# Start addresses of two activation tensors, act_a and big, modulo 64 bytes of a partition

## The reference

```python
u = rms_norm(h, ln_mix_pre[l])
hq, hf, hi, hg, aq, ak, av = jnp.split(u @ w_in[l], split_at, axis=-1)
...
mixed = jnp.concatenate([o_rec, o_att], axis=-1) @ w_out[l]
h = h + rms_norm(mixed, ln_mix_post[l])
y = conv_gated_mlp(rms_norm(h, ln_ffn_pre[l]), w_up[l], conv_w[l], conv_b[l], w_down[l])
h = h + rms_norm(y, ln_ffn_post[l])
h = h + (p[l] @ w_pe[l]) * jax.nn.sigmoid(h @ w_pg[l])
```

## Time and profile before

| what | value |
|---|---|
| executions | 1771.39, 1771.07, 1771.08 us, median 1771.08 |
| span of the profiled execution | 1769.3 us; the page gives no other time of it |
| median less span | 1.8 us |
| TensorE busy | 1755.0 us, 99% |
| VectorE, ScalarE, GpSimd busy | 1254.6, 942.8, 612.6 us |
| moved by DMA | 326.61 MB, mean 185 GB/s |

### The profile page before, as it was taken

One profiled execution on the slowest core, in us unless ns is written; L12 is line 12 of the kernel. 1 busy time (PEld: TensorE's weight loads), 2 busy tenths in 40 slices (PEclk: granted clock), 3 DMA queues, 4 the chain that ended last, 5 costly groups with the idle time before them and its releaser, 6 DMA issues.

```text
span 1769.3 us, 29586 instructions
## 1 busy us (share of the span) xinstructions
PE 1755.0 (99%) x10201; PEld 1543.0 (87%) x10201; DVE 1254.6 (71%) x1594; ACT 942.8 (53%) x1254; POOL 612.6 (35%) x621
## 2 busy tenths in 40 slices
PE   9999999999999999999999999999999999999997
PEld 7888888888888888888888888888888888888886
DVE  6877777765598777777777644444987788887754
ACT  5544554554476555555555533334655567775532
POOL 1743345556603333111111322221262255550032
PEclk9999999999999999999999999999999999999999
DMA  8444444436565555555555555556455444444453
GB/s 314 176 177 167 165 167 167 167 143 247 184 237 189 189 190 190 190 190 190 190 190 190 169 190 186 194 185 220 168 190 202 167 167 167 167 167 163 169 188 119
DMA packets 51152, 326.61 MB, mean 185 GB/s; under 512 B 5792, under 2 KB 6432, under 8 KB 18464
## 3 DMA queue, kind: packets, MB, share of 16 engines
q1 hardware_dynamic: 49952, 323.86, 50.9%
q10 hardware_dynamic: 1152, 2.11, 0.4%
HBM read 323.85 MB, written 2.10 MB: 184 GB/s over the span
## 4 chain that ended last, share of the span: by engine, by line
PE 97%; DVE 1%; ACT 1%; DMA 0%; issue 0%; ACTq 0%; DVEq 0%
PE ps L1844 59%; PE ps L1845 30%; PE ps_lev L1844 1%; PE ps_sc L1883 1%; PE ps_lev L1919 1%; PE ps_lev L1969 1%; PE ps_t L1873 1%; PE ps_lev L1845 1%; DMA x_in<-in_x_turned 0%; PE bank_b L1974 0%; DVE wlo L993 0%; PE bank_a L1888 0%; DVE o_out L1702 0%; PE bank_a L1894 0%; PE ps_t L2190 0%; ACT whi L480 0%
## 5 line engine op out<-in xcount | busy, mean ns | idle before, releaser
L1844 PE MATMUL ps<-act_a,whi 128*128 128x512 f32 x3056 | 1069.4, 394 | 0.0
L993 DVE TENSOR_TENSOR wlo<-stage,whi 128x2048 fp32r<-128x2048 f32 (+1 forms) x314 | 689.0, 2195 | 245.8 <-ACT whi L480 240.9
L1845 PE MATMUL ps<-act_a,wlo 128*128 128x256 f32 x3056 | 854.3, 280 | 0.0
L1844 PEld LDWEIGHTS ps<-act_a,whi 128*128 128x128 f32 x3056 | 573.8, 188 | 125.6 <-issue 1.0
L480 ACT ACTIVATE whi<-stage 128x2048 fp32r<-128x2048 f32 (+1 forms) x314 | 565.9, 1802 | 122.6 <-DMA stage<-in_w_down 105.0
L1845 PEld LDWEIGHTS ps<-act_a,wlo 128*128 128x128 f32 x3056 | 574.0, 188 | 0.4
L1844 PE MATMUL ps<-big,whi 128*128 128x512 f32 x1536 | 534.4, 392 | 0.0
L1845 PE MATMUL ps<-big,wlo 128*128 128x256 f32 x1536 | 429.3, 280 | 0.0
L487 ACT ACTIVATE small<-ps 128x256 f32<-128x256 f32 x240 | 91.9, 383 | 533.3 <-PE ps L1845 533.2
L1844 PEld LDWEIGHTS ps<-big,whi 128*128 128x128 f32 x1536 | 288.4, 188 | 63.4
L1845 PEld LDWEIGHTS ps<-big,wlo 128*128 128x128 f32 x1536 | 288.4, 188 | 0.1
(11 more groups left out here) (378 smaller groups left out, 1354.5 us busy)
## 6 DMA issues: line engine op xcount, KB each, us to landing
stage<-in_w_a SPq DMA_DIRECT2D x166, 1024.0 KB, 4.8
stage<-in_w_b SPq DMA_DIRECT2D x86, 1024.0 KB, 4.8
stage<-in_w_down SPq DMA_DIRECT2D x64, 704.0 KB, 4.0
stage<-in_w_a SPq DMA_DIRECT2D x8, 256.0 KB, 8.7
mem_raw<-in_memT SPq DMA_DIRECT2D x1, 2048.0 KB, 9.3
mem_again<-in_memT SPq DMA_DIRECT2D x1, 2048.0 KB, 9.1
x_in<-in_x_turned ACTq DMA_DIRECT2D x7, 256.0 KB, 9.4
x_in<-in_xT SPq DMA_DIRECT2D x3, 512.0 KB, 5.8
```

The source lines that it names most:

```text
L993: dve.tensor_tensor(wlo[:, slot, part], stage[:, slot, part], whi[:, slot, part].bitcast(F32), ALU.subtract).then_inc(w_lo, 1)
L1844: pe.matmul(dst, whi[:, slot, c * P:(c + 1) * P], act, start=start, stop=False)
L1845: return pe.matmul(dst[:, T:2 * T], wlo[:, slot, c * P:(c + 1) * P], act[:, 0:T], start=False, stop=stop)
```

## The change

The start of `act_a` is rounded up to 64 bytes: it moves from 106272 to 106304 (1661 x 64). `big` becomes a view into a row with 16 bytes of padding on either side, and moves from 139040 to 139088 (2173 x 64 + 16). `big_at`, on which the tensors laid over `big` stand, moves from 139040 to 139104, 64 bytes on, so these keep their place modulo 64; only `mem_raw` and `xg` are laid 32 bytes lower and go from 32 to 0 modulo 64. What lies over `act_a` moves with it, from 32 to 0. The end is 229216 of 229344. No instruction, wait or order changes.

```diff
--- before.py
+++ after.py
@@ -148,16 +148,17 @@
         upb = over("upb", conv_at, 0, [P, 2, T + 2])
         cy = over("cy", conv_at, 2080, [P, 2, T])
         gl = over("gl", conv_at, 4128, [P, T])
-        at[0] = conv_at + 4128 + 1024
+        at[0] = (conv_at + 4128 + 1024 + 63) // 64 * 64
         a_at = at[0]
         act_a = sb("act_a", [P, KT, 2 * T], F32R)
-        big_at = at[0]
-        big = sb("big", [P, FT, 2 * T], F32R)
+        big_row = sb("big", [P, 8 + FT * 2 * T], F32R)
+        big = big_row[:, 4:4 + FT * 2 * T].rearrange("p (k t) -> p k t", t=2 * T)
+        big_at = at[0] - 4 * FT * 2 * T
         KB = 1024
 
 
-        mem_raw = over("mem_raw", big_at, 0, [P, KT, T])
-        xg = over("xg", big_at, 16 * KB, [P, KT, T])
+        mem_raw = over("mem_raw", big_at - 32, 0, [P, KT, T])
+        xg = over("xg", big_at - 32, 16 * KB, [P, KT, T])
         warm = over("warm", big_at, 85 * KB, [P, 2 * T], BF16)
         squares = over("squares", big_at, 64 * KB, [P, KT, T])
         xs_mix = big[:, 0:KT, :]
```

## The result

The changed kernel takes 1798.7 us (median of 4 runs, 1798.45 to 1798.92), the kernel before 1771.24 (4 runs). The ratio is 1.0154, with a 95% interval of 1.0142 to 1.0166: slower by 27.5 us. The prediction said 1740.3 and a range up to 1798.

What follows compares the result with a forecast made beforehand. TensorE's matmul pairs were taken to bound the kernel. From a 1769.3 us span, 30.8 us for `act_a` and 0 for `big` left 1738.5, plus 1.8 to the median: 1740.3 us, range 1676 to 1798.

Steps and rivals of the forecast that it cites:

- What bounds the kernel: Whole kernel: TensorE, busy 1755.0 of 1769.3 us and hardly waiting; 4672 matmul pairs at 346.7 ns make 1620 us.
- The excess: Pairs on `act_a` and `big`: 19.7 ns each over 327 ns, 92.0 us in all, that a start address could bear on.
- `act_a` from 32 to 0: Pairs on `act_a`: no 64-byte piece is cut, half the excess goes, 9.85 ns a pair, 30.4 us gained.
- the sixteen matmuls of line 2190 under 233 ns: 512-column matmuls on `act_a`: a pace below 233 ns each was named as a sign of the forecast.
- `big` from 32 to 16: 1584 pairs on `big`: pieces still straddle a border, so 0; bounds 31.2 us of gain or loss.
- Everything laid over them: VectorE and ScalarE work on the moved tensors: no cost of place found, so no change.
- the DMA: The 2 MB DMA into `mem_raw`: stays at a multiple of 32, so nothing changes.
- `xg`: Half-speed float32 streams on `xg`, moved to 0: pace stays about 215 ns, so nothing changes.
- what is late next: Up projection: VectorE's share rises from 78% to 80%, weights need 194 GB/s; TensorE stays the bound, the whole saving arrives.
- the one on the slower side: Pairs on `big` at 16: with 32-byte reads its excess doubles, `act_a` keeps its pace, 1802 us; chance 0.24.
- The rule of 16-byte lines: SBUF reads: 32, 0 and 16 all start a line, so the change gives 1771 us; cited for no effect, chance 0.29.

Runs made afterwards that it cites:

- e3: Kernel before with `act_a` and `big` 64 bytes on, to 96 modulo 128, weights left at 0: 1799.37 us, ratio 1.0158.
- e11: Kernel before with everything 64 bytes on, weights at 64 and `act_a` and `big` at 96 modulo 128: 1771.21 us, ratio 0.9999.
- e9: Kernel before with padding that puts `stage` and `wlo` at 32 modulo 128, `whi` staying at 0, `act_a` and `big` at 32: 1772.6 us.
- e10: Kernel before with padding that puts `whi` at 32 modulo 128, `wlo` staying at 0, `act_a` and `big` at 32: 1800.4 us.
- e8: Kernel before with `act_a` at 40 and `big` at 36 modulo 128, weights at 0: 1805.7 us.
- e12: Kernel before with padding that puts `stage` and `wlo` at 64 modulo 128, `whi` staying at 0, `act_a` and `big` at 32: 1784.3 us.

## Why the prediction was wrong

*What bounds the kernel*: right. TensorE's starts are the time, its waits stayed at 3 us, and the pairs, 27.7 us longer in all, make up the change in span.

*The excess*: there is one, and it is tied to place. But it has no floor of zero for a good start: 346.7 ns at distance 32 was the best pace that any of the layouts tried held for all stages, though single stages ran at 340.0 and 343.3 in others, so none of these places had anything to give the kernel before. The rows could not show this, since every fast stream in them had the same places. The prediction took as bounds "0" and the whole excess and left a loss to the rivals; an effect that no row shows at a second place needed a loss within the bounds of the main term.

*`act_a` from 32 to 0*: this step failed. It took 9.85 ns a pair of gain (30.4 us) for starting on a border of 64 bytes; measured is a loss of 6.4 ns a pair in unbroken runs, 19.3 us over all pairs. Pieces of 64 bytes stand in no row and showed in no run: at 96 the pace is 353.3 as at 64, and at 64 it is 346.7 once the weights are at 32. What counts is the place against that of the weights, which the prediction didn't consider, although a load of weights stands beside every matmul in the profile. The sign that it named on the side, the sixteen matmuls of line 2190 under 233 ns, did not come either: they take 3.73 us in both kernels, though `act_a` moved.

*`big` from 32 to 16*: 0 was taken; it is a loss of 5.4 ns a pair, 8.4 us over all pairs.

*Everything laid over them, the DMA, `xg`, what is late next*: as said, within 4 ns an instruction.

*The rivals*: the one on the slower side named 1802 and came within 4 us, for a reason that falls. It kept `act_a` unchanged and doubled `big`'s excess; in truth two thirds of the loss are `act_a`'s. That part of the excess changes on one address "without it" (117.3 and 118.7 ns) was read as a small disturbance; by the experiments it looks like the thing itself, one of several paces taken at the start of a run.

*The range* ended at 1798, 0.7 us short, because it cut off the slower rival at its upper end.

The rule of 16-byte lines that the prediction set against itself (the Trainium skill, SBUF — State Buffer, Specifications) would have made no difference between starts that are multiples of 16; 32, 48, 64 and 96 gave 346.7, 350.0, 353.3 and 353.3 ns with the weights at 0, so the measurement decides against that use of it. The same skill says (TensorE: Matmul & The Clock Gate, Step-by-step: what each phase is for) that loading the next tile's weights doesn't take read bandwidth from the running matmul. The runs e3 and e11, and e9 and e10, speak against that for float32r at full rate: the place of the weights is worth 6.7 ns a pair with the moving tensors at the same bytes. That it is a clash of the two reads is the plainest reading, argued and not shown: no run leaves out the load of weights, and where ScalarE and VectorE write `whi` and `wlo` moved with the weights.

## What to carry to other kernels

Where float32r pairs fill TensorE, the distance between the moving tensor and the weights was worth up to 2% of the time here (1771.2 against 1805.7 us), with no wait and no other sign in the profile than the distance between starts. Measure that distance over a thousand matmuls, try a few paddings of 32 bytes, and keep the layout's places against each other when anything is moved; 64 bytes ahead of the weights moved all alike and cost nothing (e11), 64 between weights and activations cost 28 us (e3). Judge each stage by itself, since one layout can hold several paces, and trace more than one execution where the two distances differ, since the pace can too.

## What was not expected of the hardware

The paces come in steps: 340.0, 343.3, 346.7, 350.0, 353.3 and 360.0 ns are 816, 824, 832, 840, 848 and 864 cycles at 2.4 GHz, multiples of 8; but 348.0, 351.1, 352.0 and 355.0 occur too. These four are means of a pattern that repeats over a few pairs: from 600 us on, e8's pairs start 351, 364, 354 and 351 ns apart and then the same again, 1420 ns for four, and e12's 358, 344, 352, 353 and 353, 1760 ns for five. These sums are multiples of 8 cycles again, 3408 and 4224. A pace holds over more than a thousand pairs without drift, whatever VectorE, ScalarE and the DMAs do beside it. Plain float32 matmuls, which take a column in two cycles, keep 216 ns for 256 columns at either place. Starts that are no multiple of 16 bytes cost most over a whole kernel: 1805.7 us.
